# Attention in groups of two heads and one sequence, with the values as the stationary operand

## The reference, cut to what matters

```python
scores = (einsum('bqhd,bkhd->bhqk', qn, k_nope) + einsum('bqhr,bkr->bhqk', qp, k_pe)) * scale
p = softmax(scores, axis=-1)
return einsum('bhqk,bkhd->bqhd', p, v)          # then reshaped to 512 features a token
...
mixed = concatenate([rmsnorm(att, att_out_norm), rmsnorm(lru, lru_out_norm)], axis=-1)
x = x + mixed @ w_out
```

## Time and profile before

| what | us |
|---|---|
| median of 3 runs | 818.6 (809.74 to 821.13) |
| the profiled execution, whole | 818.04 |
| its span, first to last instruction | 816.2 |
| PE busy in the span | 690.6 (85%) |
| DVE busy | 402.2 (49%) |
| ACT busy | 260.0 (32%) |
| POOL busy | 149.1 (18%) |
| attention, first scores to the first output projection | 220 to 329 |
| output projection and routing | 329 to 441 |
| experts | 441 to about 780 |

### The profile page before, as it was taken

One profiled execution on the slowest core, in us unless ns is written; L12 is line 12 of the kernel. 1 busy time (PEld: TensorE's weight loads), 2 busy tenths in 40 slices (PEclk: granted clock), 3 DMA queues, 4 the chain that ended last, 5 costly groups with the idle time before them and its releaser, 6 DMA issues.

```text
span 816.2 us, 11266 instructions
## 1 busy us (share of the span) xinstructions
PE 690.6 (85%) x3926; PEld 459.6 (56%) x3926; DVE 402.2 (49%) x814; ACT 260.0 (32%) x493; POOL 149.1 (18%) x116
## 2 busy tenths in 40 slices
PE   2899899999899999999945996978778777788874
PEld 2788777875377678788833553434444343444431
DVE  4761798399956566587866321311211221211316
ACT  4616677636556467312110110111101011100113
POOL 5330943019103323000002010010000001000041
PEclk9999999999989699999965999999989999988998
DMA  6799310300510000332286999999999999999977
GB/s 191 213 225 208 84 52 1 110 1 26 209 50 1 1 1 2 142 116 104 104 323 256 418 419 421 421 418 419 419 419 421 421 420 418 419 419 422 414 262 295
DMA packets 60325, 197.61 MB, mean 242 GB/s; under 512 B 8192, under 2 KB 21632, under 8 KB 50048
## 3 DMA queue, kind: packets, MB, share of 16 engines
q1 hardware_dynamic: 47264, 162.53, 52.4%
q0 software_dynamic: 4896, 17.83, 5.7%
q10 hardware_dynamic: 8128, 16.78, 5.5%
HBM read 169.86 MB, written 27.26 MB: 242 GB/s over the span
## 4 chain that ended last, share of the span: by engine, by line
PE 40%; DMA 20%; SPq 16%; DVE 15%; issue 4%; ACT 3%; POOL 1%; POOLq 0%; ACTq 0%; DVEq 0%
DMA ring<-in_w_up 16%; SPq L443 9%; PE bank L648 9%; PE bank L803 8%; SPq L449 6%; PE bank L691 4%; PE bank L853 4%; PE bank L710 4%; PE bank L878 2%; PE bank L700 2%; DVE ring L1449 2%; PE bank L766 1%; DVE ring L1425 1%; PE bank L611 1%; DMA ring<-expert_rows,pos_i 1%
## 5 line engine op out<-in xcount | busy, mean ns | idle before, releaser
L853 PE MATMUL bank<-ring,tmp 128*64 128x256 f32 x896 | 119.5, 428 | 48.0 <-DMA ring<-in_w_up 47.1
L853 PEld LDWEIGHTS bank<-ring,tmp 128*64 128x64 f32 x896 | 71.3, 155 | 101.3 <-issue 43.6
L648 PE MATMUL bank<-u_high,w_high 128*128 128x256 f32 (+3 forms) x224 | 79.0, 353 | 6.3 <-POOL w_low L495 3.2
L1149 ACT ACTIVATE rope<-bank 64x256 f32<-64x256 f32 x40 | 15.1, 378 | 210.2 <-PE bank L853 210.2
L1587 DVE SCALAR_TENSOR_TENSOR rope<-rope,bank 64x256 f32<-64x256 f32 x40 | 16.6, 415 | 128.9 <-ACT rope L1149 128.2
L648 PE MATMUL bank<-u_low,w_high 128*128 128x256 f32 (+3 forms) x224 | 76.0, 339 | 0.0
L648 PE MATMUL bank<-u_high,w_low 128*128 128x256 f32 (+3 forms) x224 | 75.9, 339 | 0.0
L1597 DVE COPY rope<-bank 128x128 f32<-128x128 f32 x40 | 11.7, 292 | 123.8 <-PE bank L864 123.8
L853 PE MATMUL bank<-mix,tmp 128*64 128x256 f32 x384 | 47.1, 403 | 11.1 <-DMA mix<-in_w_up 11.1
L878 PE MATMUL bank<-ring,rope 128*64 128x512 f32 x224 | 54.2, 605 | 0.0
L1154 ACT ACTIVATE mix<-bank 128x512 f32<-128x512 f32 x40 | 23.9, 598 | 89.1 <-PE bank L878 89.1
(11 more groups left out here) (256 smaller groups left out, 1194.2 us busy)
## 6 DMA issues: line engine op xcount, KB each, us to landing
ring<-in_w_up SPq DMA_DIRECT2D x28, 1024.0 KB, 25.8
ring<-in_w_down SPq DMA_DIRECT2D x28, 1024.0 KB, 26.9
ring<-in_w_gate SPq DMA_DIRECT2D x28, 1024.0 KB, 23.7
mix<-in_w_gate SPq DMA_DIRECT2D x12, 1024.0 KB, 23.2
mix<-in_w_up SPq DMA_DIRECT2D x12, 1024.0 KB, 25.7
mix<-in_w_down SPq DMA_DIRECT2D x12, 1024.0 KB, 26.6
expert_rows<-mix ACTq DMA_DIRECT2D x80, 128.0 KB, 7.2
expert_rows<-norm_row SPq DMA_DIRECT2D x1, 7168.0 KB, 41.8
```

The costliest lines, as they stand in the source:

```text
L648: last = pe.matmul(psum[u % ZB][0:m, 0:tn], w[:, t % W_RING, k, 0:m], x[:, k, t0:t0 + tn], start=(k == 0 and p == 0), stop=(k == DC - 1 an ...
L853: last = pe.matmul(psum[q][t * WB:(t + 1) * WB, 0:F], xT[:, j, c, q * WB:(q + 1) * WB], w[:, (t * DC + c) * F:(t * DC + c + 1) * F], start ...
```

## The change

Attention goes by **groups** of two heads and one sequence, sample first: 8 groups, of 8 steps (four tiles, two heads) or 4 (two tiles, two heads). The exponentials are scaled by one over the row sum while they lie in SBUF (`normed`), before they are transposed; the transposed blocks of a whole group are collected, and then one `values(at)` multiplies: the value columns of a head (128 x 64) are stationary, the probabilities of all queries of the sequence move (512 or 256 columns), and the two heads write the two halves of the partitions of one bank. The result is feature-major, so the transposes of `att` at the end go away. The squares for the output norm are now taken by group on ACT, added up over the head pairs by POOL (`add_heads`), and summed over the features by six matmuls (`square_sums`). There are four score banks and four `prob` buffers; PE runs three scores ahead. The residual rows are loaded when attention is over, since their place now holds probabilities. Part 1 of slot 3 is loaded behind part 0, since its place now holds a split row of `w_out`.

```diff
+        groups = [(pair, tiles) for pair in range(NH // 2) for tiles in (range(PROMPT // P, NT), range(PROMPT // P))]
+        steps = [(2 * pair + k, i, at) for at, (pair, tiles) in enumerate(groups) for k in range(2) for i in tiles]
+        ends = [max(n for n, step in enumerate(steps) if step[2] == at) for at in range(len(groups))]
+        SCORE_BANKS = (0, 1, 2, 7)
...
 SP
-            sp.wait_ge(g("gh"), 8)
-            load_res(0)
-            load_res(1)
...
-            sp.wait_ge(g("pv"), len(steps))
-            load_part(3, 3, 1)
+            sp.wait_ge(g("pv"), len(groups))
+            load_res(0)
+            load_res(1)
             load_part(3, 3, 2)
...
             load_part(3, 3, 0)
+            load_part(3, 3, 1)
...
 POOL
-            for j in (LC, LC + 1, LC + 2, LC + 3):
-                split_rows(j)
-            for c in range(LC):
-                split_branch(c)
+            def add_heads(at):
+                ...
+                po.wait_ge(g("asq"), at + 1)
+                po.tensor_tensor(att_ssq[:, t], att_ssq[:, t], att_sq[:, at % 2, 0:len(tiles) * P], ALU.add).then_inc(g("aqs"), 1)
+            split_rows(LC)
+            split_rows(LC + 1)
+            add_heads(2)
+            add_heads(3)
+            split_rows(LC + 2)
+            split_rows(LC + 3)
+            add_heads(4)
+            split_branch(0)
+            split_branch(1)
+            add_heads(5)
+            add_heads(6)
+            split_branch(2)
+            split_branch(3)
+            add_heads(7)
...
 PE
             def turn(n):
-                pe.wait_ge(g("pr"), n + 1)
+                pe.wait_ge(g("nrm"), n + 1)
...
+            def values(at):
+                pe.wait_ge(g("pTe"), ends[at] + 1)
+                if at >= 2:
+                    pe.wait_ge(g("atT"), at - 1)
                 for b in range(kn // P):
+                    for k in range(2):
+                        h = 2 * pair + k
+                        last = pe.matmul(psum[5 + at % 2][k * VH:(k + 1) * VH, 0:kn],
+                                         V[:, k0 // P + b, h * VH:(h + 1) * VH], turned_of(at)[:, b, k, :],
+                                         start=(b == 0), stop=(b == kn // P - 1))
...
             for n in range(len(steps)):
-                if n + 2 < len(steps):
-                    scores(n + 2)
+                if n + 3 < len(steps):
+                    scores(n + 3)
                 turn(n)
-                if n >= 1:
-                    values(n - 1)
+                if n - 1 in ends:
+                    values(ends.index(n - 1))
...
+            def square_sums():                       # ahead of the first attention half of the projection
+                pe.wait_ge(g("asq"), len(groups))
+                pe.wait_ge(g("aqs"), len(groups) - 2)
+                for i in range(NT):
+                    last = pe.matmul(psum[0][:, i:i + 1], att_ssq[:, i * P:(i + 1) * P], ones[:, 0:1], ...)
...
 ACT
+            def att_high(at):
+                ac.wait_ge(g("pv"), at + 1)
+                ac.activation(square, psum[5 + at % 2][:, 0:kn], ACT.Square).then_inc(g("asq"), 1)
+                ac.activation(at_high[:, pair, t], psum[5 + at % 2][:, 0:kn], ACT.Copy).then_inc(g("ath"), 1)
             for n in range(len(steps)):
-                if n + 1 < len(steps):
-                    exps(n + 1)
+                if n + 2 < len(steps):
+                    exps(n + 2)
                 pt_out(n)
+                if n - 2 in ends:
+                    att_high(ends.index(n - 2))
...
 DVE
+            def normed(n):
+                v.wait_ge(g("pr"), n + 1)
                 link(v.reciprocal(rr[:, k:k + 1], rs[:, k:k + 1]))
-                v.wait_ge(g("pv"), n + 1)
-                v.tensor_scalar(att[:, i, h * VH:(h + 1) * VH], psum[5][:, 0:VH], rr[:, k:k + 1], None, ...
+                v.tensor_scalar(prob[:, k, 0:kn], prob[:, k, 0:kn], rr[:, k:k + 1], None, ALU.mult).then_inc(g("nrm"), 1)
...
+            def att_low(at):
+                v.wait_ge(g("ath"), at + 1)
+                v.tensor_tensor(at_low[pair][:, t], psum[5 + at % 2][:, 0:kn], at_high[:, pair, t].bitcast(f32),
+                                ALU.subtract).then_inc(g("atT"), 1)
...
             for n in range(len(steps)):
-                if n + 2 < len(steps):
-                    maxes(n + 2)
-                if n >= 1:
-                    att_out(n - 1)
+                if n + 1 < len(steps):
+                    normed(n + 1)
+                if n + 3 < len(steps):
+                    maxes(n + 3)
...
+                if n - 2 in ends:
+                    att_low(ends.index(n - 2))
                 if n - 1 in ROWS_AT:
                     rows_low(ROWS_AT[n - 1])
```

More of the change, by code:

```diff
@@ L730, in _ @@
             scores(1)
+            scores(2)
+            pe.wait_ge(g("lrs"), 2)
             for n in range(len(steps)):
-                if n + 2 < len(steps):
-                    scores(n + 2)
+                if n + 3 < len(steps):
+                    scores(n + 3)
                 turn(n)
-                if n >= 1:
-                    values(n - 1)
-                if n - 3 >= len(steps) - NT:
-                    turn_att(n - 3 - (len(steps) - NT))
-            values(len(steps) - 1)
-            for i in range(NT - 3, NT):
-                turn_att(i)
+                if n - 1 in ends:
+                    values(ends.index(n - 1))
+            values(len(groups) - 1)
+            def square_sums():
+                pe.wait_ge(g("asq"), len(groups))
+                pe.wait_ge(g("aqs"), len(groups) - 2)
+                for i in range(NT):
+                    last = pe.matmul(psum[0][:, i:i + 1], att_ssq[:, i * P:(i + 1) * P], ones[:, 0:1], start=(i == 0),
+                                     stop=(i == NT - 1), skip_group_check=True)
+                last.then_inc(g("asp"), 1)
             pe.wait_ge(g("wout"), 16)
@@ L793, in _ @@
                         if k == 1:
-                            pe.wait_ge(g("atT"), i + 1)
+                            pe.wait_ge(g("atT"), len(groups))
+                            if i == 0 and half == 0:
+                                square_sums()
                             if half == 0 and i >= 1:
@@ L1076, in pt_out @@
             def pt_out(n):
-                kn = keys(steps[n][1])[1]
+                h, i, at = steps[n]
+                kn = keys(i)[1]
+                q0 = (i - groups[at][1][0]) * P
                 ac.wait_ge(g("pT"), n + 1)
-                if n >= 2:
-                    ac.wait_ge(g("pv"), n - 1)
-                ac.activation(probT[:, n % 2, 0:kn], psum[3 + n % 2][:, 0:kn], ACT.Copy).then_inc(g("pTe"), 1)
+                back = 2 if at % 2 else 4
+                if at >= back:
+                    ac.wait_ge(g("pv"), at - back + 1)
@@ L1094, in att_squares @@
[L1094 to L1098 removed]
+            def att_high(at):
+                pair, tiles = groups[at]
+                kn = len(tiles) * P
+                t = slice(tiles[0] * P, tiles[0] * P + kn)
+                ac.wait_ge(g("pv"), at + 1)
+                if at >= 4:
+                    ac.wait_ge(g("aqs"), at - 3)
+                square = att_ssq[:, t] if at < 2 else att_sq[:, at % 2, 0:kn]
+                ac.activation(square, psum[5 + at % 2][:, 0:kn], ACT.Square).then_inc(g("asq"), 1)
+                ac.activation(at_high[:, pair, t], psum[5 + at % 2][:, 0:kn], ACT.Copy).then_inc(g("ath"), 1)
@@ L1504, in _ @@
                                            op0=ALU.mult, op1=ALU.mult).then_inc(g("ln"), 1)
-                if n - 4 >= len(steps) - NT:
-                    att_low(n - 4 - (len(steps) - NT))
+                if n - 2 in ends:
+                    att_low(ends.index(n - 2))
                 if n - 1 in ROWS_AT:
                     rows_low(ROWS_AT[n - 1])
-            att_out(len(steps) - 1)
-            for i in range(NT - 4, NT):
-                att_low(i)
+            att_low(len(groups) - 1)
             v.wait_ge(g("asd"), 1)
```

129 lines of the change are left out of this document (54 added, 75 removed).

## The result

The changed kernel takes 819.2 us (median of 20 runs, 817.9 to 822.1), the kernel before, run beside it, 816.6 (20 runs, 808.9 to 823.8). The ratio is 1.0081, 95% interval [1.0063, 1.01]: 0.8% slower, where 0.6% faster was forecast. The ratio leaves out runs over 1.5% above the fastest of their kernel, five of the 20 before and none after; over all runs the medians are 0.3% apart. The profiled execution took 819.35, its span 817.5, against 818.04 and 816.2.

A forecast was written before the change was run, and what follows sets the result against it. PE was taken to bound attention before, with VectorE's 70.0 us close to PE's 75.6 afterwards. The first projected half 6.7 us earlier and the moved load 2.5 later gave -4.2 against 818.04: 814 us, 8-in-10 range 798 to 836.

The forecast's parts named there:

- PE: right: PE's work in attention: 75.6 us against 90.3 before, 14.7 less, with the product's two output halves overlapping.
- the third rival: Products of the values: the halves don't overlap, 18 us more of PE, 832 us in all; chance 0.04.
- the end of attention: Last values end at 319.4 us, POOL's last split at 323.5, first projected half at 328.2, 6.7 us earlier than before.
- POOL's hold: Scalings on VectorE held up beside POOL's splits in attention: 6 us, between bounds of nothing and 18.
- The scaling: VectorE's new 128x512 scaling in each long step: 0.42 us, taken as 0.34 from start to start.
- Waits: VectorE without work behind the products at group boundaries: 4.6 us a head pair, 16.2 in all.
- The slow clock at the start: Start of attention: the lower granted clock costs PE some 4 us, as before.
- The last transposes, copy and product: End of attention, after VectorE's last steps: 1.7 us until the last values end.
- The moved load: Experts' stage: loading part 1 of slot 3 behind part 0 costs 2.5 us.
- the fourth rival: Experts' stage: the moved load is hidden, 811 us in all; chance 0.04.
- PE did not set the pace (798): Denies the first rival: in attention PE still sets the pace, its saving shows in full, 20.3 us less; chance 0.17.
- The half-clock rival: Attention: PE's gaps repeatedly halve the granted clock for some 14 us, 7 us each; 835 us; chance 0.12.

The follow-up runs named there:

- e3: The changed kernel with all eight POOL splits put behind the last sample group's addition, `add_heads(6)`; 837.8 us in all, one execution.
- e1: The changed kernel with VectorE taking the rest of a group's result (`att_low`) one step later, behind the next scaling; 819.0 us, ratio 1.0055.
- f3: The changed kernel with e1's edit and POOL's last two branch splits ahead of the addition of group 6; 812.4 us, ratio 0.9969.
- e2: The changed kernel with part 1 of slot 3 loaded early again, behind the first two experts; 817.25 us, ratio 1.0031.
- h2: The changed kernel with two transposes of every step done twice on PE; 821.1 us, ratio 1.0094.
- i1: f3 with e2's load, and VectorE's weight rows and branch scalings moved to where it waits behind sample products; 801.6 us, ratio 0.9811.
- e4: The kernel before with VectorE's four branch scalings in steps 1 to 4 instead of 5, 13, 21 and 29; 804.1 us, ratio 0.9877.

## Why the prediction was wrong

**PE: right.** The eight matmuls of a sample group, 16 instructions in the trace, take 3.65 us (3.6 priced), the four of a prompt group 1.08 (0.9): the halves overlap and the third rival (832) is out. PE is busy 93.7 us between 220 and 336, before 109.2.

**The step that failed is the end of attention**: the last values were to end at 319.4 and end at 325.9, and the first half misses 328.2 by as much, 6.4 us. That the stretch between the two came out as priced, 8.6 us against 8.8, is luck: it was added up through POOL's last split, which was to end at 323.5 and set the end; that split ended at 327.2, and PE did not wait for it, but was held by its own product and the 1.2 GHz level behind it. VectorE was to be through its steps at 317.7 (319.4 less the last 1.7); its last scaling ends at 322.81. From 223.07, these 99.7 us are: steps 32 x 1.38 + 16 x 0.98 = 59.8; seven rests 3.4; rows 4 x 1.19 = 4.8; branch scalings 3.7; held by POOL 21.4 + 10.9 less 32 x 0.49 + 16 x 0.35, 11.0; waits 15.4; 1.6 without a releaser. Against the priced terms:

- *POOL's hold*: 11.0 us of longer scalings, against 6 priced and 18 as the upper bound. The Trainium skill, "SBUF — State Buffer", section "SBUF: two separate sides", has VectorE and GpSimd exclude each other for a whole instruction; the scaling of 2.37 us beside POOL's 3.20 agrees, and the rule at full length for every split (18) remains too much. The term counted only the second instruction of a split; the first holds too (0.94 us at 321.87, beside a CAST). Some 3.9 of the 11.0 stand in the last short steps of the first two head pairs, and there VectorE waits 1.48 and 1.58 us for the score behind the product, in place of 3.47 in the third, where nothing was held (3.1 priced): that part fell into a wait. By e3, 2.7 us of the hold, in one execution, reached the end of the product.
- *The scaling*: 0.49 us alone, 0.40 to the next start. I took 0.34, from the nearest row, one of 128x771 that had waited for POOL. But the 0.42 by which that one ended behind POOL is not a scaling's length: with 512 columns it is 0.28 or 0.29. 48 steps make it 2.7 us.
- *Waits*: 15.4 us against 16.2: right in sum, wrong in place. The last sample group's were to be 2.4 and are 4.50: no step was left for VectorE beside that product, and its rest stood ahead of the last scaling. By e1, in one execution, the place of the rests in the list, there and at the other groups, cost 5.7 us of the product's end.
- *The slow clock at the start* (4) is no term of its own on VectorE; it is in the waits.
- *Smaller terms*: rows and branch scalings 8.5 us in place of 7.4, which was 8.9 less 1.5 for waits that they were to fill; rests 3.4 in place of 4.0; 1.6 without a releaser was not priced.
- *The last transposes, copy and product* (1.7) took 325.9 - 322.8 = 3.1, at the lower clock, behind a gap of 3.01 us.

So VectorE's list is 5.1 us longer than priced, and what follows it 1.4: the mechanism of the sum held, and its terms for the hold, the scaling, the last wait and the end were too small. Per head pair I had priced about 20 us; between the sample products at 238.63 and 315.62 there are three pairs, 25.7 us each. e1 and f3 test the end: with the rests behind the scalings and POOL's last splits one place ahead, the first half stands at 330.32, 4.2 of the 6.4 us earlier; by the medians f3 is 6.8 us under the changed kernel.

**The moved load: right in kind**, 2.0 us by e2 (2.5 priced); the fourth rival (811) is out.

**The rivals.** PE did not set the pace (798): it idles over 20 us. Its argument, that PE's saving shows in full, fails by h2, where 10.6 us put back on PE cost 1 to 2. The half-clock rival (835) has its mechanism, not its size: the granted clock fell in four places (224 to 232, 284 to 288, 312 to 316, 320 to 332 us), none of them 14 us long. What the clock takes, (1 - clock) x 4 us over the slices below 1.00, is about 9 us after and 10 before, so it explains no part of the 1.3 us between these two executions.

**What I did not see** is what follows from pacing by turns. The sum had it: VectorE's list, plus its waits for PE's bursts, and the kind of the account held. But the rows and scalings stand in VectorE's own turns, from 250 to 258 us for example, and there PE waits for them, while VectorE's waits behind the products lay unused. i1 moves all of it into these waits and comes out some 10 us earlier, though its clock was also better. And the base was not free of a cost of its own: the kernel before loses 10 us to where four scalings stand (e4).

## What to carry over

When work is taken from the engine that sets the pace, ask which engine paces each stretch afterwards: here two engines with like sums and a short look-ahead paced by turns, and the stage took 99.7 us on VectorE where either engine's work was priced at 70 to 76. Then move the other engine's loose work to where it waits; the same instructions in another place came with 10 us less here, twice (e4, i1). An instruction that waits for something late belongs behind those that others wait for.

## What was not expected of the hardware

A gap does not tell whether the granted clock falls behind it, nor for how long. At the start of attention PE waits 1.92 us in the kernel before and in e4, which run the same instructions up to there. PE before, then in e4:

```profile
224.35 0.53 PE L700 MATMUL bank<-consts,softm 128*128 128x128 f32 x2 [1.92 <-ACT softm L1073]
```

```profile
223.54 0.44 PE L700 MATMUL bank<-consts,softm 128*128 128x128 f32 x2 [1.92 <-ACT softm L1073]
```

From 224 to 228 us the clock is 0.57 before and 1.00 in e4. Later, before, a gap of 1.88 us led to some 14 us at or near 0.50; after, one of 3.37 us led to one slice at 0.57, and the next stands at 1.00.

A scaling that met POOL ended just behind POOL's instruction, all twelve times after the change: 0.15 us behind it with 256 columns, 0.28 or 0.29 with 512, whether POOL ran a CAST, a subtraction or an addition. The scaling at 263.75 ends at 265.55, POOL's split at 265.40; the one at 282.36 ends at 284.73, POOL's at 284.45; the one at 321.87 at 322.81, POOL's CAST at 322.66.
